# Retention and the last output projection as one stage, head by head, with each step's output product in two halves

## The reference

```python
def step(S, inp):                      # retention, chunks of 128 tokens
    qc, kc, vc = inp
    o_inter = jnp.einsum('bhtk,bhkv->bhtv', qc, S) * q_decay
    scores = jnp.einsum('bhtk,bhsk->bhts', qc, kc) * intra_decay[None]
    o_intra = jnp.einsum('bhts,bhsv->bhtv', scores, vc)
    S_new = chunk_decay * S + jnp.einsum('bhsk,bhsv->bhkv', kc * k_decay, vc)
    return S_new, o_inter + o_intra
...
q, k, v, g = jnp.split(h @ w_in, SPLITS_ODD, axis=-1)
...
o, s_new = retention_chunk_scan(q, k, v, log_gamma, s0, chunk)
o = rms_norm(o).reshape(b, t, W_C) * jax.nn.silu(g.astype(f32))
return o.astype(h.dtype) @ w_out, s_new
...
yp = yp + op
ys = ys + os_
```

## Time and profile before

| | us |
|---|---|
| median of three runs | 2333.31 |
| lowest, highest | 2330.46, 2337.14 |
| the profiled execution | 2327.28 |
| its span in the profile | 2325.2 |
| mean granted TensorE clock in it | 0.915 of 2.4 GHz |
| TensorE busy | 1992.4 (86%) |
| VectorE busy | 897.6 (39%) |
| ScalarE busy | 531.7 (23%) |
| GpSimd busy | 659.7 (28%) |

### The profile page before, as it was taken

One profiled execution on the slowest core, in us unless ns is written; L12 is line 12 of the kernel. 1 busy time (PEld: TensorE's weight loads), 2 busy tenths in 40 slices (PEclk: granted clock), 3 DMA queues, 4 the chain that ended last, 5 costly groups with the idle time before them and its releaser, 6 DMA issues. The chain is left out here.

```text
span 2325.2 us, 28346 instructions
## 1 busy us (share of the span) xinstructions
PE 1992.4 (86%) x10186; PEld 1578.0 (68%) x10186; DVE 897.6 (39%) x1336; ACT 531.7 (23%) x989; POOL 659.7 (28%) x550
## 2 busy tenths in 40 slices
PE   5999999778887837886948999999999588986999
PEld 4789998644444526764838999887888455555786
DVE  5640000277874449762246443111000156554110
ACT  3210100256654332322121000000111244332000
POOL 2422230056551026522022332222330122216000
PEclk9999999898889967877979999999999789997999
DMA  4332231323323650114443243222321689866320
GB/s 134 111 98 80 77 105 47 113 84 90 117 90 97 199 178 2 58 59 145 149 140 95 75 117 106 80 83 80 98 84 43 205 277 303 291 223 245 109 81 27
DMA packets 205240, 278.75 MB, mean 120 GB/s; under 512 B 27284, under 2 KB 145492, under 8 KB 201812
## 3 DMA queue, kind: packets, MB, share of 16 engines
q1 hardware_dynamic: 130420, 183.79, 25.0%
q10 hardware_dynamic: 72256, 84.70, 11.0%
q0 software_dynamic: 2464, 8.91, 1.1%
HBM read 186.91 MB, written 88.08 MB: 118 GB/s over the span
## 5 line engine op out<-in xcount | busy, mean ns | idle before, releaser
L241 PE MATMUL odd_bank<-odd_w_hi,odd_h_hi 128*128 128x512 f32 (+1 forms) x576 | 224.5, 390 | 1.1 <-DVE odd_stage_tm L453 1.1
L241 PE MATMUL odd_bank<-odd_w_lo,odd_h_hi 128*128 128x512 f32 (+1 forms) x576 | 224.4, 389 | 0.0
L241 PE MATMUL odd_bank<-odd_w_hi,odd_h_lo 128*128 128x512 f32 (+1 forms) x576 | 224.1, 389 | 0.0
L1699 PE MATMUL out_bank<-out_w_hi,out_m_hi 128*128 128x512 f32 (+1 forms) x432 | 136.8, 399 | 54.0 <-DVE out_w_lo L1769 47.6
L222 POOL CAST odd_w_hi<-odd_raw 128x1024 fp32r<-128x1024 f32 x48 | 53.3, 1110 | 399.3 <-PE odd_bank L241 333.7
L1699 PE MATMUL out_bank<-out_w_hi,out_m_lo 128*128 128x512 f32 (+1 forms) x432 | 135.6, 395 | 0.0
L1699 PE MATMUL out_bank<-out_w_lo,out_m_hi 128*128 128x512 f32 (+1 forms) x432 | 135.4, 395 | 0.0
L1699 PEld LDWEIGHTS out_bank<-out_w_hi,out_m_hi 128*128 128x128 f32 (+1 forms) x432 | 80.2, 187 | 75.2 <-issue 48.1
L241 PE MATMUL odd_bank<-odd_h_hi,odd_w_hi 128*128 128x362 f32 (+1 forms) x384 | 127.9, 333 | 1.5 <-DVE odd_h_lo L424 1.5
L241 PE MATMUL even_bank<-even_h_hi,even_w_hi 128*128 128x362 f32 (+1 forms) x384 | 126.2, 329 | 1.6 <-DVE even_stage_tm L453 1.6
L241 PE MATMUL odd_bank<-odd_h_hi,odd_w_lo 128*128 128x362 f32 (+1 forms) x384 | 127.3, 332 | 0.0
(11 more groups left out here) (274 smaller groups left out, 4068.5 us busy)
## 6 DMA issues: line engine op xcount, KB each, us to landing
odd_raw<-in_w_in_odd SPq DMA_DIRECT2D x48, 512.0 KB, 4.0
even_raw<-in_w_in_even SPq DMA_DIRECT2D x32, 512.0 KB, 4.0
k_page<-in_cache_k SPq DMA_DIRECT2D x64, 256.0 KB, 3.1
v_page<-in_cache_v SPq DMA_DIRECT2D x64, 256.0 KB, 3.0
rt_s<-in_state_ret SPq DMA_DIRECT2D x32, 512.0 KB, 6.0
out_ret_sample<-rt_s ACTq DMA_DIRECT2D x32, 512.0 KB, 4.8
v_tm<-odd_stage_tm ACTq DMA_DIRECT2D x64, 128.0 KB, 1.9
g_tm<-odd_stage_tm ACTq DMA_DIRECT2D x64, 128.0 KB, 1.9
```

Source lines behind the costliest of these rows:

```text
L241: mm = pe.matmul(out, stationary, moving, start=(j == 0), stop=(j == len(pairs) - 1))
L1699: mm = pe.matmul(bank[slot][n][0:r, :], m, w[:, c, n * 512:n * 512 + 512], start=(c == 0 and j == 0), stop=(c == K - 1 and j == 2))
```

## The change

project_out("out1") and retention become one stage, retention_out. retention only keeps its arguments; the output projection of the even layer stays as it was.

- The order is head outside and chunk inside: n = 8h + c. Only one state is held, and step n's state product follows the update of step n-1. It is stored at a head's end, and VectorE waits for that store (state_left) before it starts the next one.
- q and k lie in HBM by head (by_head instead of by_chunk), and are loaded by the step, as are v and g, in three buffers each.
- The samples are done by head: at c = 2 and c = 6, four sequences of one head (sample_outputs), straight from qd_s, with 4 opening products each time; o0 or o1 takes the result, and tr gets its 32 wanted columns by a float32 product with the selection matrix pick. There are 8 sample units, where there were 2. A unit's index m counts steps and sample units, in order.
- Mix stays on the chip. ScalarE rounds tr to m_hi (round_mix), VectorE subtracts to m_lo (split_mix), and only then tr is free: turn_out waits for m_split.
- w_out of one head (4 rows) is held at a time, as w_hi and w_lo; ScalarE, VectorE and GpSimd make the next head's in step 8h + 1.
- y1 is loaded to SBUF once (nine tiles) and the four heads' products are added to it there, in two banks y0 and y1 of 512 columns each. The product of step n-2's tile stands in step n: its first half between turn_out or sample_outputs and the sample state products, the second half behind them. The sample tile follows in steps 8h + 8.
- sc and kt share a bank, and scores(n) waits for kd_split alone; kd_hi is made after scm_done; the square goes into og, and norm waits for tr_done for that; all stack calls but the first come in steps 0 to 3, two in each.
- Stores of states and of y, and all loads, are SP's; ScalarE has the loads of the tables, now in parts, and the stack's.

```diff
-def by_chunk(x):
+def by_head(x):
...
-        sc, kt = ps("sc", [P, P]), ps("kt", [P, J, P])
+        sckt = ps("sckt", [P, P + J * P])
...
+        yp = [ps("y0", [P, 512]), ps("y1", [P, 512])]
...
+                sp.wait_ge(s1_done, J * (n + 1))
+                sp.dma_start(state_samples[c, h].rearrange("(j k) v -> k j v", k=P), s1[n % 2][:]).then_inc(s1_left[n % 2], 16)
...
+                if c == NCH - 1:
+                    sp.wait_ge(state_done, J * (n + 1))
+                    sp.dma_start(state_prompt[h].rearrange("(j k) v -> k j v", k=P), state[:]).then_inc(state_left, 16)
...
             def turn_out(m):
 
                 pe.wait_ge(gated, m + 1)
                 if m:
-                    pe.wait_ge(tr_read, m)
-                for c in range(DV // P):
-                    mm = pe.transpose(tr[:, c, :], og[:, m % 2, c * P:c * P + P], ident)
+                    pe.wait_ge(m_split, m)
+                for r in range(R):
+                    part = og[:, m % 2, r * P:r * P + P]
+                    if units[m][0] == "step":
+                        mm = pe.transpose(tr[:, r, :], part, ident[:])
+                    else:
+                        mm = pe.matmul(tr[:, r, 0:ROWS], part, pick[:], start=(r == 0), stop=True, skip_group_check=True)
                 mm.then_inc(tr_done, 1)
...
+            def product_out(h, t, halves=range(2)):
+
+                n_out, rows = out_of[h, t], rows_of(t)
+                m = unit_of["step", h * NCH + t] if t < NCH else unit_of["samples", h * NGRP + 1]
+                pe.wait_ge(m_split, m + 1)
+                hi, lo = (m_hi[:, t % 2], m_lo[:, t % 2]) if t < NCH else (ms_hi[:], ms_lo[:])
+                for half in halves:
+                    cols = slice(half * 512, half * 512 + 512)
+                    if n_out:
+                        pe.wait_ge(added, 2 * (n_out - 1) + half + 1)
+                    for r in range(R):
+                        if half == 0 and t == 0:
+                            pe.wait_ge(w_split_p if r % 2 else w_split_d, R // 2 * h + r // 2 + 1)
+                        for j, (a, b) in enumerate(((hi, w_hi), (hi, w_lo), (lo, w_hi))):
+                            mm = pe.matmul(yp[half][0:rows, :], a[:, r, :], b[:, r, cols], start=(r == 0 and j == 0),
+                                           stop=(r == R - 1 and j == 2))
...
                 if n + 2 < NSTEP:
                     scores(n + 2)
-                for m in turned_in(n):
-                    turn_out(m)
...
+                for x in turned_in(n):
+                    if units[x][0] == "samples":
+                        pe.wait_ge(picked, SEQS)
+                    turn_out(x)
+                if c % SEQS == 2:
...
+                    sample_outputs(h, c // SEQS)
+
+                first, *others = outs_in(n) or [None]
+                if first:
+                    product_out(*first, range(1))
+                if n < NCH:
+                    pe.wait_ge(stacked[n], NSTACK)
...
+                if first:
+                    product_out(*first, range(1, 2))
+                for x in others:
+                    product_out(*x)
...
-            def norm(m, src):
+            def norm(m):
 
                 at = slice(m % 2, m % 2 + 1)
-                if m:
-                    act.wait_ge(sq_done, m)
+                act.wait_ge(o_done, m + 1)
                 if m >= 2:
-                    act.wait_ge(gated, m - 1)
-                nc.scalar.activation(square[:], src, ACT.Square, accum_out=ss[:, at]).then_inc(sq_done, 1)
+                    act.wait_ge(tr_done, m - 1)
+                nc.scalar.activation(og[:, m % 2, :], o[m % 2][:], ACT.Square, accum_out=ss[:, at]).then_inc(sq_done, 1)
...
+            round_weights(0)
             for n in range(NSTEP):
...
+                norm(unit_of["step", n])
+                for seq in range(2 * n + 1, min(2 * n + 3, NS)):
+                    stack(seq)
                 if n + 2 < NSTEP:
                     prepare(n + 2)
                 for m in turned_in(n):
-                    store(m)
-                if n:
-                    store_state(n - 1)
+                    round_mix(m)
+                if n % SEQS == 2:
+                    norm(unit_of["samples", n // SEQS])
+                if n > NCH and n % NCH == 1:
+                    round_weights(n // NCH)
...
+                for m in turned_in(n):
+                    split_mix(m)
+                dve.wait_ge(s0_in[c % SEQS], 16 * (n // SEQS + 1))
...
+                for x in outs_in(n):
+                    add(*x)
+                if n > NCH and n % NCH == 1:
+                    split_weights(n // NCH)
```

More of the change, by code:

```diff
@@ L1851, in retention @@
         v_rows, g_rows = (t.rearrange("t (h n) -> t h n", n=DV) for t in (v_tm, g_tm))
-        NCONST, NSTACK = 32, 16 * 6
+        w_rows = weight.rearrange("(c p) n -> p c n", p=P)
+        NCONST, NSTACK, NFIRST = 16 * 6, 16 * 6, 3
         units = []
         for n in range(NSTEP):
-            units.append(n)
-            if n % GSTEP == GSTEP - 1:
-                units.append(None)
-        unit_of = {n: m for m, n in enumerate(units) if n is not None}
-        last_of = [m for m, n in enumerate(units) if n is None]
+            units.append(("step", n))
+            if n % SEQS == 2:
+                units.append(("samples", n // SEQS))
@@ L1863, in turned_in @@
+        unit_of = {x: m for m, x in enumerate(units)}
+        outs = [(n // NCH, t) for n in range(NSTEP) for t in ((6, NT - 1) if n % NCH == 6 else (n % NCH,))]
+        out_of = {x: i for i, x in enumerate(outs)}
         def turned_in(n):
@@ L1866, in turned_in, with outs_in, qd_until @@
                 return []
-            return [unit_of[n - 1]] + ([last_of[(n - 1) // GSTEP]] if n % GSTEP == 0 else [])
-        def left_until(m):
-            return sum(16 * (HC if units[x] is None else 1) for x in range(m) if x % 2 == m % 2)
+            more = [unit_of["samples", (n - 1) // SEQS]] if (n - 1) % SEQS == 2 else []
+            return [unit_of["step", n - 1]] + more
+        def outs_in(n):
+            return [] if n < 2 else [x for x in outs if x[0] == (n - 2) // NCH and x[1] == (n - 2) % NCH or
+                                     (n - 2) % NCH == 6 and x == ((n - 2) // NCH, NT - 1)]
+        def qd_until(n):
+            return n - n // NCH
         def stack_rows(seq, part):
@@ L1964, in scores @@
             def scores(n):
[L1965 to L1972 removed]
+                pe.wait_ge(qk_in[n % NQ], 32 * (n // NQ) + 32)
                 if n:
@@ L1975, in scores @@
                 for j in range(J):
-                    mm = pe.transpose(kt[:, j], k[:, c % 2, h, j], ident)
+                    pe.matmul(sc, k[:, n % NQ, j], q[:, n % NQ, j], start=(j == 0), stop=(j == J - 1))
+                for j in range(J):
+                    mm = pe.transpose(kt[:, j], k[:, n % NQ, j], ident[:])
                 mm.then_inc(kt_done, 1)
@@ L2066, in _ @@
         @block.scalar
         def _(act):
+            flat = lambda x: x.rearrange("p a b -> p (a b)")
+            tables = consts["ret_p"]
+            at = 0
+            for dst, n in ((ident[:], P), (flat(decay[:]), HC * P), (flat(q_dec[:]), HC * P), (flat(q_dec_s[:]), HC * TS), (None, NS * TS), (k_dec[:], HC)):
+                if dst is not None:
+                    act.dma_start(dst, tables[:, at:at + n]).then_inc(const_in, 16)
+                at += n
             act.dma_start(table_s[:], consts["ret_s"]).then_inc(const_in, 16)
-            act.dma_start(table_p[:], consts["ret_p"]).then_inc(const_in, 16)
@@ L2129, in _ @@
             act.wait_ge(smp_v, 16)
[L2130 removed]
+            nc.scalar.copy(vs_hi, v_s[:]).then_inc(first_vs_hi, 1)
             prepare(0)
```

447 lines of the change are left out of this document (249 added, 198 removed).

## The result

The kernel after takes 2364.84 us (median of four runs, 2359.79 to 2370.58), 1.0134 times the kernel before, with a 95% interval of 1.0106 to 1.0161. In a second set of six runs it took 2364.67, a ratio of 1.0141 (1.0104 to 1.0177). The forecast was 2341, slower, with a range of 2304 to 2369: the sign and the range held, the size did not. The change costs 31 us where 8 were forecast, and the time lies in the band that the prediction had given to its slower rival (2353 to 2375).

The account below looks back on a forecast made before the run. TensorE's work, 389 us standing in 474, was taken as the bound. 1914 + 367 + 29 + 12 + 3 = 2325 against 2320.0, plus 2 unpriced and 1 for the last store, is +8: 2341 us, range 2304 to 2369.

Parts of the forecast that it names:

- slower rival: In each of 32 steps, VectorE's order puts a further 1 us on TensorE, s1 waiting for stores: 2369; chance 0.2.
- first load to step 0: Ahead of the retention's steps: step 0 begins about 1 us later than at 1846.25, as scores(1) wait for kd_split(0).
- steps 0 to 3: The start: ScalarE stacks two sequences a step, 11.1 us a step; 30 of 66 us lost, step 3 ending at 1914.
- pauses in steps 7 to 31: TensorE idle at the samples' turn in every fourth step: six times 4.4 us, 2.7 in step 31, sum 29.
- lower clock behind them: Behind each double-turn pause half the matmul rate is lost for a while: seven times 1.7 us, 12.
- heads' first steps: Where a head changes, VectorE waits for the prompt state's store, behind others on SP's queue: 1 us each, 3 in all.
- sample steps: Steps with sample outputs: openings at 1.0 each, +6; turning by selection at 0.8, +5; forecast 7 x 14.05.
- the rest, with 2 unpriced and 1 at the end: Added to the sum: 2 us for waits not priced, 1 for a last store of a full 512 KB tile.
- three parts: Of the double turn's pause: norm's wait for the transposes +1.2, the kt cast in the chain +0.4, VectorE's subtraction +0.7.
- signs: In the profile after: 7 or 8 TensorE waits for mix's split, 4 us each, 25 to 35 in all; VectorE 60% busy.
- The faster one: At the double turn: the wait is short, giving 2300, decided at a pause of about 3 us each; chance 0.25.
- The third, a shorter start: At the start: stack's DMAs overlap more and step 4 starts at 1905, time 2332; within the forecast's own spread.

Follow-up runs that it names:

- the late turn: Against the kernel after, the samples' turn and VectorE's split for it go to the end of the step, behind both output product halves: 2305.94 us, 0.9903 of before.
- the tables first: Against the kernel after, SyncE waits for the tables before the second chunk's loads; raw weights come earlier, y and samples' g in step 1: 2365.56 us.
- the halves together: Against the kernel after, both halves of the output product go behind the sample state's product: 2354.79 us, and 2357.72 in a second set.

## Why the prediction was right in sign and short in size

The terms of the sum against what the kernel after shows, from the stage's first load; the forecast, 8 us above before, is a stage of 506.1, the measured one is 532.1:

| term | forecast | measured | difference |
|---|---|---|---|
| first load to step 0 | 20.4 | 25.9 | +5.5 |
| steps 0 to 3 | 66.5 | 74.3 | +7.8 |
| pauses in steps 7 to 31 | 29 | 29.7 (6 x 4.46 + 2.95) | +0.7 |
| lower clock behind them | 12 | 20.3 (6 x 2.83 + 3.3) | +8.3 |
| heads' first steps | 3 | 7.0 (3 x (17.32 - 15.0)) | +4.0 |
| sample steps | 7 x 14.05 | 7 x 14.32 | +1.9 |
| the rest, with 2 unpriced and 1 at the end | | | -2.2 |
| sum | 506.1 | 532.1 | +26.0 |

(The 3.3 of step 31: 34.92 less 29.47 of the late turn is 5.45, and 0.83 that the late turn waits itself, less the pause of 2.95.)

**Right.** The work: plain steps take 11.25 us, where 11.2 was forecast, and 28 us of idle TensorE went. The pause is 4.46 us where 4.4 was forecast, 2.95 where 2.7 was, and in step 3 8.67 where 8 was. Of its three parts the square's wait was tested alone: taking it away gave back 1.3 (forecast 1.2). The other two stand in the rows of step 15: from ScalarE's start on kd to its start on scm 0.38 (forecast 0.4), from the start of the split to the next product 0.84 (forecast 0.7). This one wait decides the sign: without it the kernel is 1.0% faster than before. The prediction's own figure for that case, 2300, is close to the 2305.94 measured, but in part by luck: it takes 41 us away where the late turn took 57, from a sum that was 24 too low. VectorE is no bound: 6.18 us busy in the plain step of 11.25 at 1937.04 (60% was forecast). The waits for the split are 38.4 us in all, above the 25 to 35 of its signs, since step 3 is among them.

The sign had some luck too. A forecast of 8 us stood just above the 7 that the prediction said it could tell, it gave slower no more than 0.45, and the measured time is 4 us from the end of the range. That the sign came out so clearly is due to terms that nearly all came out too small.

**Mis-sized.** First, the clock. The prediction took the smaller of its two rows, 1.7 of 1.7 to 2.75, and the pauses here cost 2.83 each; the shorter pauses of 3.15 us cost 2.8 as well. The larger bound was the one that came true: in step 15 the tensor engine stays at 1.2 GHz for 6.6 us, where the two stretches of before had 3.5 and 5.5. (The Trainium skill, "TensorE: Matmul & The Clock Gate", section "HAM oscillation — how this bites in real kernels", says that a kernel whose matmuls stop again and again pays the clock's transition each time. The traces agree. Its example has 1.67 us at half rate for each pause, so an estimate from that page would be 0.8 us a pause and 6 us for seven; the trace has 2.8 each in the mean.)

Second, the start. The prediction priced ScalarE's twelve issues at 8.0 a step by a row of 0.67 each. Here they keep ScalarE from its next work for 9.2, 10.9 and 10.9 us, since two or three of the twelve take 1.1 to 2.2 instead of 0.63; that is 7.0 more than three times 8.0, near the 7.8 by which steps 0 to 3 are longer. Two of the three:

```profile
1875.40 0.63 ACTq L2226 DMA_DIRECT2D rt_v_stack<-rt_y  x1
...
1880.07 1.07 ACTq L2226 DMA_DIRECT2D rt_v_stack<-rt_y  x1
1881.24 0.62 ACT L2185 CAST rt_v_hi<-rt_v 128x512 fp32r<-128x512 f32 x1 [9.22 <-issue]
...
1885.40 2.23 ACTq L2226 DMA_DIRECT2D rt_v_stack<-rt_y  x1
...
1894.45 0.62 ACT L2185 CAST rt_v_hi<-rt_v 128x512 fp32r<-128x512 f32 x1 [10.88 <-issue]
```

And the tables land later, which the prediction did not ask about at all. They are issued by 1839.7, and TensorE starts at 1850.47, 13.7 us behind the first load, where it started 8.0 behind it before (1835.11). That is all of the +5.5; what follows up to step 0 takes 12.2 instead of 11.1, the 1 us that was forecast. TensorE's first product, in after and then before, and a stretch of after:

```profile
1850.47 1.97 PE L2103 MATMUL rt_u<-rt_s 128*64 128x64 f32 x16 [18.33 <-DMA rt_table_s<-table_ret_s]
```
```profile
1835.11 1.97 PE L2011 MATMUL rt_u<-rt_q_s,rt_k_s 128*64 128x64 f32 x16 [12.70 <-DMA rt_table_p<-table_ret_p]
```
```profile
1842.00:1850.00 8.00, 0.00 (x0) 0.00 (x0) 0.00 (x0) 0.00 (x0) 0.00 (x0) 0.50 1.01 207
```

With a DMA share of 1.01 only 207 GB/s are moved. Before, the same time behind the first load (1832.06 to 1840.06) had 320 GB/s at 1.02, and in the 3 us from 1832 on 407. The same bytes come in smaller pieces: 5746 packets for 11.13 MB in the first 40 us, where before had 3379 for 11.57 MB. The loads behind the tables are little of it: with the tables first, when nothing but them and the first six loads is under way, TensorE still starts 12.0 us behind the first load, so they account for 1.7 of the 5.7. The rest lies with the tables and those first loads. The tables are now six loads instead of two, and the one waited for is issued last, 2.4 us behind the first load, where before both were issued within 0.6; q, k and v come by chunk and head, v a quarter as wide. Which of these it is was not tested.

Third, the heads' first steps. The prediction named the right wait (the prompt state's store, behind others on SyncE's queue) and gave it 1 us. It is 4.79 for VectorE, of which the first half of the output product hides all but 0.37; a wait of 1.2 for the additions follows where the sample tile's product begins. The rest of the 2.3 each was not taken apart.

**The cover that the forecast gave to the half.** "The wait for VectorE's state addition (1.4 us behind u) lies under the first half" is not borne out: nothing is lost without it, with the halves together plain steps take 11.22. Where it does cover something is the store at a head's change, and only when nothing else gives that store time.

**The rivals.** The faster one asked for a short pause; the pause is not short. The slower one's mechanism, VectorE late with stores in every step, isn't there: no wait for a state store comes back each step. The time fell into its band from other terms. The third, a shorter start, is refuted with the start's +13.3.

## What to carry to other kernels

When a wait depends on a chain that begins on the waiting engine itself, move the waiting instruction behind work that does not depend on the chain, and not only the chain's pieces: moving the samples' turn and its subtraction to the end of the step gave 57 us of the stage, shortening the chain by 1.3 us gave 11. Price every pause with its clock, and by the larger of the rows at hand. A gain measured beside a pause belongs to that pause: measure it again once the pause is gone, before adding it to anything.

## What the runs showed of the hardware

A pause of TensorE of 3.15 us cost as much clock as one of 4.46 (2.8 us each in the mean of six, 1.9 to 3.5 in single steps), and the clock can fall after the engine has resumed: 0.97 for 2.3 us, then 0.50. Twelve issues of 32 and 64 KB copies held ScalarE for 9.2 to 10.9 us, but GpSimd for 6.0 (1862.68 to 1868.63), and neither way the start was shorter. A load of 128 KB took 30.6 us to land when 24 such copies were issued behind it on GpSimd, and 12.0 in the kernel after, where ScalarE issues them.
